# Hybrid decoder layer: the memory probabilities' turned copy gets a buffer of its own, and VectorE's small steps of the mix stage change places

## What is computed

```
h = rmsnorm(x); sq, sk, sv, gq, gk, gv, gg, glr, mq = split(h @ w_in)
# A: 8 query heads, 2 key heads, window 128; bias by distance, a learned sink per head
m = max(max(scores), sink); p = exp(scores - m)
p = p / (sum(p) + exp(sink - m)); y_swa = p @ v
# B: gated linear attention, 4 heads: decayed state, per-head norm, swish gate
# C: 4 heads over 256 memory tokens
p = softmax(q k / 8); y_mem = p @ v
x += concat(y_swa, y_gla, y_mem) @ w_out
```

## Time and profile before

| | us |
|---|---|
| median of 3 runs | 1716.83 |
| the profiled execution | 1716.92 |
| its span | 1715.1 |
| PE busy | 1698.6 (99%) |
| DVE busy | 1124.3 (66%) |
| ACT busy | 726.9 (42%) |
| POOL busy | 548.0 (32%) |

### The profile page before, as it was taken

The page is one execution under the profiler, slowest core; times in us unless marked ns, Lnnn a source line. Parts: engine busy times, 40 slices in busy tenths (PEclk is TensorE's granted clock), DMA queues, the critical chain, the costliest instruction groups (busy, mean ns, idle before and its releaser), DMA issues.

```text
span 1715.1 us, 24899 instructions
## 1 busy us (share of the span) xinstructions
PE 1698.6 (99%) x8329; PEld 1389.2 (81%) x8329; DVE 1124.3 (66%) x1575; ACT 726.9 (42%) x1367; POOL 548.0 (32%) x448
## 2 busy tenths in 40 slices
PE   9999999999999999999999999999999999999999
PEld 6788888888888889888866688888888888888887
DVE  7975555555499696248878863985555555569754
ACT  5533333333344463243267822543333333344442
POOL 0454445544130141012156612145554444310000
PEclk9999999999999999999999999999999999999999
DMA  7342222233774431120100122222233322484434
GB/s 206 71 151 95 93 103 92 102 112 120 275 241 132 160 99 68 49 86 25 37 2 2 39 98 99 74 99 92 94 108 122 110 104 92 171 284 159 137 103 166
DMA packets 101694, 191.71 MB, mean 112 GB/s; under 512 B 11491, under 2 KB 13972, under 8 KB 101612
## 3 DMA queue, kind: packets, MB, share of 16 engines
q1 hardware_dynamic: 100528, 188.48, 32.2%
q0 software_dynamic: 848, 2.10, 1.0%
q10 hardware_dynamic: 236, 0.06, 0.0%
HBM read 139.74 MB, written 50.86 MB: 111 GB/s over the span
## 4 chain that ended last, share of the span: by engine, by line
PE 92%; DVE 3%; ACT 1%; POOL 1%; issue 1%; DVEq 0%; ACTq 0%
PE ps L56 29%; PE ps L57 29%; PE ps L58 29%; PE ps L1695 1%; PE ps L1623 1%; ACT glu L1828 1%; POOL Pg L1995 1%; DVE loT L376 1%; PE ps L1613 1%; PE ps L1744 0%; DVE ring L505 0%; PE ps L1732 0%; PE ps L1417 0%; PE ps L1414 0%; PE ps L1718 0%
## 5 line engine op out<-in xcount | busy, mean ns | idle before, releaser
L505 DVE TENSOR_TENSOR ring<-w_raw,ring 128x512 fp32r<-128x512 f32 x240 | 240.2, 1016 | 219.1 <-ACT ring L500 219.0
L56 PE MATMUL ps<-hiT,ring 128*128 128x512 f32 x672 | 261.5, 389 | 1.6 <-DVE ring L505 1.6
L58 PE MATMUL ps<-hiT,ring 128*128 128x512 f32 x672 | 261.4, 389 | 0.0
L57 PE MATMUL ps<-loT,ring 128*128 128x512 f32 x640 | 249.0, 389 | 0.0
L56 PE MATMUL ps<-down_ring 128*128 128x512 f32 x616 | 239.6, 389 | 0.0
L57 PE MATMUL ps<-down_ring 128*128 128x512 f32 x616 | 239.6, 389 | 0.0
L58 PE MATMUL ps<-down_ring 128*128 128x512 f32 x616 | 239.6, 389 | 0.0
L56 PE MATMUL ps<-hiB,ring 128*128 128x512 f32 x576 | 224.9, 390 | 0.0
L58 PE MATMUL ps<-hiB,ring 128*128 128x512 f32 x576 | 224.1, 389 | 0.0
L500 ACT ACTIVATE ring<-w_raw 128x512 fp32r<-128x512 f32 x240 | 150.6, 629 | 165.2 <-PE ps L58 160.4
L879 ACT ACTIVATE down_ring<-down_raw 128x512 fp32r<-128x512 f32 x176 | 108.9, 630 | 225.5 <-DMA down_raw<-act_dram 185.1
(11 more groups left out here) (269 smaller groups left out, 3039.2 us busy)
## 6 DMA issues: line engine op xcount, KB each, us to landing
down_raw<-act_dram SPq DMA_DIRECT2D x154, 256.0 KB, 2.6
w_raw<-in_w_gate SPq DMA_DIRECT2D x88, 256.0 KB, 3.1
w_raw<-in_w_up SPq DMA_DIRECT2D x88, 256.0 KB, 3.2
act_dram<-actT SPq DMA_DIRECT2D x88, 256.0 KB, 2.0
act_dram<-act SPq DMA_DIRECT2D x66, 256.0 KB, 2.0
wd<-in_w_down SPq DMA_DIRECT2D x44, 256.0 KB, 5.1
wd_mirrored<-in_w_down SPq DMA_DIRECT2D x33, 256.0 KB, 4.5
p_raw<-in_w_proj SPq DMA_DIRECT2D x15, 512.0 KB, 3.6
```

What stands on the lines that cost most here:

```text
L56: nc.tensor.matmul(out, w_hi, x_hi, start=first, stop=False, skip_group_check=resumed)
L57: nc.tensor.matmul(out, w_hi, x_lo, start=False, stop=False, skip_group_check=resumed)
L58: return nc.tensor.matmul(out, w_lo, x_hi, start=False, stop=last, skip_group_check=resumed)
L505: nc.vector.tensor_tensor(ring[:, e % RING, 1, :], op_source(e), ring[:, e % RING, 0, :].bitcast(F32), ALU.subtract).then_inc(op_ready, 1)
```

## The change

- `PT` of unit 2 is no longer `glu` but `rstd` seen with two key tiles of 512 columns, the place where the unscaled and scaled memory probabilities lie. Its copy waits for the turn alone. The memory exponentials of a block wait for the memory values of the block before (in place of the turn). The copy of unit 0 waits for the values of unit 0 of the block before (in place of the memory values).
- `bias_max` is cut in two: the maximum, and the shift with the sink's (`bias_shift`). For unit 0 they stay together. For unit 1 the shift comes after both low halves of the block before.
- The edges of a block are made one block earlier, between the output gate and the state update.
- The denominators of unit 0 come between gating of q and the maximum of unit 1, in place of after the low halves. Those of unit 1 come between the second and the third masked copy, in place of before the first.
- Ahead of block 0 the order of instructions stays as it was.

```diff
--- before.py
+++ after.py
@@ -164,7 +164,7 @@
         square_lo = place(196 * KB, ("square_lo", [P, 2, HALF], F32R))[0]
         bias, Pg0 = place(184 * KB, ("bias", [P, SWA_HEADS, 2 * P], F32), ("Pg0", [P, 4, 2 * P], F32))
         P_of = [Pg0[:], Pg1[:], rstd[:].rearrange("p (h k) -> p h k", h=4)]
-        PT = (glu, PT1, glu)
+        PT = (glu, PT1, rstd[:].rearrange("p (t q) -> p t q", t=2))
 
         ps = ctx.enter_context(nc.psum_tensor("ps", [P, 8, HALF], F32))
         BANK_X, BANK_Y, BANK_BIAS, BANK_WARM, BANK_NORM = (0, 2), (1, 3), 4, 5, 6
@@ -1507,8 +1507,9 @@
                     unit_vector(dve, u)
                 if i == NG - 1:
                     dve.wait_ge(bias_landed, 16)
-                    bias_max(dve, 0, 0)
-                    bias_max(dve, 1, 0)
+                    for u in range(2):
+                        bias_max(dve, u, 0)
+                        bias_shift(dve, u, 0)
                     gate_edges(dve, 0)
                     denominators(dve, 0, 0)
                 dve.wait_ge(proj_ready, i + 1)
@@ -1633,6 +1634,8 @@
                 nc.vector.tensor_tensor_reduce(out=P_of[u][:, i, band(n)], in0=s, in1=bias[:, swa_head(c), band(n)], scale=1.0,
                                                scalar=sinks[:, swa_head(c):swa_head(c) + 1], op0=ALU.add, op1=ALU.max,
                                                accum_out=row_max[:, c:c + 1]).then_inc(biased, 1)
+
+        def bias_shift(dve, u, n):
             dve.wait_ge(biased, 8 * n + 4 * u + 4)
             hs = slice(4 * u, 4 * u + 4)
             nc.vector.tensor_scalar(shift[:, hs], row_max[:, hs], -1.0, None, ALU.mult).then_inc(shifted, 1)
@@ -1808,7 +1811,7 @@
 
             def mem_exps(n):
                 act.wait_ge(shifted, 5 * n + 5)
-                wait(act, turned, unit_count(2, n - 1))
+                wait(act, values_done, unit_count(2, n - 1))
                 for i in range(4):
                     c = 8 + i
                     nc.scalar.activation(P_of[2][:, i, :], ps[:, SCORE_BANK[2] + i // 2, (i % 2) * MEM:(i % 2 + 1) * MEM],
@@ -1817,12 +1820,8 @@
 
             def pt_copy(u, n):
                 act.wait_ge(turned, unit_count(u, n))
-                if u == 0:
-                    wait(act, values_done, unit_count(2, n - 1))
-                elif u == 1:
-                    wait(act, values_done, unit_count(1, n - 1))
-                else:
-                    act.wait_ge(values_done, unit_count(0, n))
+                if u < 2:
+                    wait(act, values_done, unit_count(u, n - 1))
                 tiles = key_tiles(n, u)
                 at = slice(tiles[0], 2)
                 nc.scalar.activation(PT[u][:, at, :], ps[:, TURN_BANK[u] + tiles[0]:TURN_BANK[u] + 2, :], ACT.Copy
@@ -1916,6 +1915,8 @@
                     if l:
                         dve.wait_ge(level_taken, SPLITS * n + l)
                     nc.vector.copy_predicated(to, mask, got).then_inc(level_taken, 1)
+                    if l == 1:
+                        denominators(dve, 1, n)
 
             def update_state(n):
                 dve.wait_ge(kv_ready, n + 1)
@@ -1947,20 +1948,20 @@
             mem_max(0)
             for n in range(NB):
                 more = n + 1 < NB
-                if n:
-                    gate_edges(dve, n)
                 if not more:
                     gate_out(n - 1)
-                denominators(dve, 1, n)
                 take_levels(n)
                 if more:
                     bias_max(dve, 0, n + 1)
+                    bias_shift(dve, 0, n + 1)
                 mem_denominators(n)
                 if more:
                     if n:
                         gate_out(n - 1)
+                    gate_edges(dve, n + 1)
                     update_state(n)
                     gate_q(n + 1)
+                    denominators(dve, 0, n + 1)
                     bias_max(dve, 1, n + 1)
                 else:
                     unit_vector(dve, NPROJ)
@@ -1969,7 +1970,7 @@
                 swa_lo(n)
                 mem_lo(n)
                 if more:
-                    denominators(dve, 0, n + 1)
+                    bias_shift(dve, 1, n + 1)
                     mem_max(n + 1)
 
         def mix_pool(pool):
```

## The result

The changed kernel takes 1727.89 us (median of 4 runs, 1725.42 to 1728.23) against 1716.80 on the same chip: 11.1 us longer, ratio 1.007, interval 1.0055 to 1.0086. The forecast was 1718.2; the time is close to that of the rival with the stuck denominators, 1727.2. The profiled execution took 1727.96 us, its span 1726.1 against 1715.1.

What follows compares the result with a forecast made beforehand. TensorE, busy 1698.6 of 1715.1 us, was taken to bound the kernel. 0.97 + 3.05 - 2.40 - 0.33 = +1.3 on the profiled 1716.92 gave 1718.2 us; own range 1716.9 to 1720.3, outer range 1715.0 to 1728.0.

Steps and rivals of the forecast that it cites:

- the rival with the stuck denominators: In blocks 2 to 7, the early sink add waits 1.97 us behind GpSimd's gating of k: 9.0 us, 1727.2; chance 0.28.
- the slack of the early add: L1654 behind VectorE's gating of q goes ahead of GpSimd's gating of k if asked in time; slack 0.35 - 0.30 = 0.05.
- port wait: VectorE's moved second shift waits for the GpSimd scaling in flight: 0.08 us a block taken, bounds 0 to 0.45.
- Price of the stuck add: Low half comes 11.4 us behind the spans in place of 9.8: some 1.5 us a block, six blocks, 9.0 us.
- Own place: Unit 2's copy no longer waits for unit 0's values, so memory values move 0.40 us earlier; 6 x 0.40 = 2.40 gained.
- Late second shift: Second exponentials start 0.69 us later behind the low halves; less ScalarE's slack of 0.16, 0.53 us lost per block.
- Both together: Per block, the 0.40 us gained on the memory probabilities' copy against 0.53 and 0.08 lost by the second shift.
- The step into block 1: Edges beside GpSimd's diagonal delay the gatings 0.45 us, then the low half and exponentials: +0.97, bounds 0.53 to 1.4.
- Early sums free the turn of unit 0, and the scores wait for ScalarE instead: Unit 0's denominators come 3 us earlier; the turn's 0.40 us GpSimd wait goes, and ScalarE holds the scores.
- Last block, -0.33: Block 7's masked copies start earlier without edges and denominators between: 0.53 - 0.20 = 0.33 us gained.
- ScalarE isn't late: Exponentials not held by the shift; turn, scores and spans follow the levels in six blocks: -5.3 us, 1711.6; chance 0.12.
- The granted clock: The new gap ahead of the scores makes TensorE's clock fall in all six blocks: 16.5 us, 1734.7 alone; chance 0.08.

Runs made afterwards that it cites:

- early denominators alone: Kernel before, with only unit 0's denominators moved straight behind VectorE's gating of q: ratio 1.0078, blocks of 16.89 us.
- shift at once: Changed kernel with the second shift straight behind the maximum of unit 1, denominators still early: 1721.43 us, ratio 1.0040.
- the repaired kernel: Changed kernel with GpSimd's gating of k waiting for the first set's early row sums: blocks of 15.34 to 15.37 us.
- the two repaired kernels: Changed kernel with gating of k held back, or with unit 0's denominators back behind the second shift: blocks 15.34 to 15.37 and 15.30 to 15.36 us.
- the late shift alone: Kernel before, with only unit 1's shift split off and put behind VectorE's low halves: blocks of 15.77 us.
- the two tries at a better whole: Changed kernel with second shift straight behind its maxima and gating of k held back, edges early or back: neither ratio distinguishable from the kernel before.
- own place alone: Kernel before, with only PT of unit 2 and its waits changed, run twice: 1709.06 against 1714.42 us, 1711.49 against 1714.38.
- the second pair: Kernel before with only unit 0's denominators early, without and with GpSimd's gating of k held back: blocks 16.89 and 15.23 us.

## Why the prediction was wrong

**The step that failed** is the slack of the early add: "If L1654 asks before 908.23 it goes first, as VectorE's pairs do now", then "0.05, less the 0.08 of port wait: a knife's edge", and a chance of 0.28. It was wrong twice. First, the sum wasn't followed. The slack came out as worked out: -0.03 by that sum, and in the trace the operand ends 0.02 us behind the gating of q. By its own number the forecast should have had the add stuck in most blocks, and yet it put 0.48 on the other side and left the wait out of its sum. What the runs showed in its place is five adds of 1.91 to 1.93 us and blocks of 16.80; with the gating of k held back, adds of 0.15 or 0.16 and blocks of 15.35. Second, the rule under the number was false: with 0.69 us to spare (early denominators alone), and with the operand ready 0.48 and 0.08 us ahead (shift at once), GpSimd's waiting instruction still went first. No row of before bore the rule out. Behind the gating of q stood the biased maxima, one of whose inputs is in PSUM, and the earlier trace rows, the one row of an add beside GpSimd, showed it waiting.

The other steps, each with its measured size:

- *Price of the stuck add:* 1.5 us a block forecast on top of the sum; measured 16.80 - 15.35 = 1.45 over the repaired kernel, and 1.52 over the kernel before. The prediction doesn't show where its 8.85 us for the end of the gating of k comes from (its rows give 910.19 - 900.98 = 9.21); it measured 912.28 - 903.49 = 8.79. The rival's 10.3 us over the profiled time of before was 9.0 for six blocks and 1.3 for the rest; the 11.0 measured are 7.6 for five blocks, 1.7 for half the clock in one, and 1.7 in all for the step into block 1, the mix's start and what follows the last spans. That the rival's time was met within 1 us is in part luck, by that exchange: it had six stuck blocks and no fall of the clock.
- *Own place:* -0.40 a block forecast, -0.41 measured alone, and the ratios say -4.1 and -2.7 us for a forecast of -2.40.
- *Late second shift:* +0.53 a block, and 0.08 for the port. Measured +0.49 alone. The shift took 0.16 us there and in the changed kernel: the port wait was nought.
- *Both together:* +0.21 forecast, +0.07 measured with the add clear (15.35), as -0.41 and +0.49 give.
- *The step into block 1:* +0.97 forecast, 16.94 against 16.12 us measured, +0.82 (16.72 and 16.67 in the two repaired kernels). Its cause, edges beside the diagonal, is not shown: the late shift alone gives +0.28 in this step, and the two tries at a better whole that differ only in the edges' place have 14.33 us with them early and 14.39 with them back.
- *Early sums free the turn of unit 0, and the scores wait for ScalarE instead:* right, 0 and 1.08 us in the block shown.
- *Last block, -0.33:* in the two repaired kernels last spans to end are 752.7 us against 753.0, but they are so in the kernel with the own place alone too, which has no such edit. Not settled.
- *ScalarE isn't late* (the faster rival): against it stand the 1.08 us that the scores wait for ScalarE and the +0.49 of the late shift alone.
- *The granted clock:* 0.08 for a fall in all blocks. It fell in one, which the rivals had only as all or none.
- *The range:* from the terms as given (no port wait and block 1 at 0.53; port wait 0.45 and block 1 at 1.4) it is 1717.4 to 1720.5, not 1716.9 to 1720.3. The outer range, up to 1728.0, holds the measured time only because it was drawn around the stuck case.

The sum without the collision, +1.3 us or a ratio of 1.0008, lies inside the intervals of both repaired kernels, and so does no change at all; from the first spans to the end their traces have +0.7 and +0.4 us. So the accounting of the chain agrees with the runs as far as they can tell, its terms being 0.14 us a block and, in the step into block 1, some 0.4 us too large, and the forecast was lost on the early add.

## What to carry to other kernels

Before a VectorE instruction with two SBUF inputs is moved, look at what GpSimd has waiting at that time: a row of 0.15 us cost nearly that instruction's whole length here, 2 us, and having its operand ready 0.69 us early didn't help. Move the small one to where GpSimd's long one has ended, or let a semaphore order the two; one wait on GpSimd gave back 1.45 us a block here, and 1.66 in the second pair. A slack of a few hundredths worked out from a trace is no slack, and when the sum falls below nought, forecast that side.

## What the runs showed of the hardware

- Where GpSimd had an instruction waiting at the end of VectorE's gating of q, GpSimd's went first, with the add's operand ready: six adds of 2.04 or 2.05 us (early denominators alone), three in the shift-at-once kernel (2.04 and 2.05, and 0.97 held by the diagonal), and four of 0.96 held by the diagonal where the gating of k was held back too. The other way round, the add held by the diagonal ended at 925.14, ahead of the gating of k that GpSimd had next (925.09 to 927.18). Whether the engines take turns or the one that has waited longer goes first, these meetings can't tell: in each, the row that went first is also the one that began first. That either is the chip's rule is a reading of these meetings, not tested further.
- The granted clock fell to half behind one of five gaps of equal length (1.56 to 1.57 us) in the changed kernel, and behind the last of six of 1.83 us with the early denominators alone. In the shift-at-once kernel it fell behind gaps of 2.42, 1.81, 2.38 and 1.52 us. So the length of the gap ahead of the levels did not decide it alone.
